# Turning the local pairs' attention probabilities with VectorE blocks and DMA instead of TensorE transposes, in a two-layer hybrid encoder kernel

## The reference

```python
s = einsum('bhcd,ibhcjd->bhcij', q_row, k_win) * scale + bias   # local attention, per grid row
p = softmax(s over the window)
ya = einsum('bhcij,ibhcjd->bhcd', p, v_win) * silu(ag)
x = x + concatenate([ya, yb, yc]) @ w_out
```

## Time and profile before

| | us |
|---|---|
| median of 3 runs | 532.09 (531.93 to 534.18) |
| the profiled execution | 532.22 |
| its span | 530.2 |
| TensorE busy in it | 519.1 (98%) |
| VectorE, ScalarE, POOL busy | 369.8, 279.3, 135.5 |
| SP's queue, POOL's queue: share of the 16 DMA engines | 17.8%, 51.6% |

### The profile page before, as it was taken

One profiled execution on the slowest core, in us unless ns is written; L12 is line 12 of the kernel. 1 busy time (PEld: TensorE's weight loads), 2 busy tenths in 40 slices (PEclk: granted clock), 3 DMA queues, 4 the chain that ended last, 5 costly groups with the idle time before them and its releaser, 6 DMA issues.

```text
span 530.2 us, 7797 instructions
## 1 busy us (share of the span) xinstructions
PE 519.1 (98%) x2846; PEld 406.2 (77%) x2846; DVE 369.8 (70%) x721; ACT 279.3 (53%) x535; POOL 135.5 (26%) x168
## 2 busy tenths in 40 slices
PE   8999999999999999999999999999999999999995
PEld 6888777587786887888888877877768678777884
DVE  6979697989984627611539969979999646546134
ACT  6713376565765558623423315756657656654314
POOL 0114232122133312324411233122122352123201
PEclk9999999999999999999999999999999999999999
DMA  8625688766675875799502479975785969669963
GB/s 285 270 79 138 158 196 203 164 168 160 151 194 137 216 176 117 182 279 269 155 6 99 108 168 217 205 174 133 169 185 137 229 163 253 133 133 231 229 139 159
DMA packets 39014, 92.32 MB, mean 174 GB/s; under 512 B 5440, under 2 KB 16960, under 8 KB 38976
## 3 DMA queue, kind: packets, MB, share of 16 engines
q0 software_dynamic: 17856, 61.09, 51.6%
q1 hardware_dynamic: 20832, 30.54, 17.8%
q10 hardware_dynamic: 288, 0.19, 0.1%
HBM read 81.84 MB, written 4.72 MB: 163 GB/s over the span
## 4 chain that ended last, share of the span: by engine, by line
PE 79%; DMA 9%; DVE 6%; issue 2%; SPq 1%; ACT 1%; POOL 1%; POOLq 0%; DVEq 0%; ACTq 0%
PE acc L560 17%; PE acc L562 17%; PE acc L561 17%; PE tp L684 5%; PE misc L703 4%; PE sc L670 4%; DMA sq<-sq 3%; DMA w_hi<-w_in 2%; DMA bias<-nabias 1%; PE sc L622 1%; PE sc L623 1%; PE sc L624 1%; DMA v_way<-vB 1%; PE sc L560 1%; PE sc L562 1%
## 5 line engine op out<-in xcount | busy, mean ns | idle before, releaser
L560 PE MATMUL acc<-act_hi,w_hi 128*128 128x512 f32 x480 | 195.2, 407 | 0.0
L562 PE MATMUL acc<-act_lo,w_hi 128*128 128x512 f32 x480 | 187.7, 391 | 0.0
L561 PE MATMUL acc<-act_hi,w_lo 128*128 128x512 f32 x480 | 187.3, 390 | 0.0
L562 PEld LDWEIGHTS acc<-act_lo,w_hi 128*128 128x128 f32 x480 | 90.1, 188 | 20.0
L560 PEld LDWEIGHTS acc<-act_hi,w_hi 128*128 128x128 f32 x480 | 90.2, 188 | 17.8 <-issue 1.4
L561 PEld LDWEIGHTS acc<-act_hi,w_lo 128*128 128x128 f32 x480 | 90.5, 188 | 17.0 <-issue 0.5
L783 ACT ACTIVATE w_lo<-w_hi 128x1024 fp32r<-128x1024 f32 (+1 forms) x62 | 61.9, 999 | 42.1 <-DMA w_hi<-w_out 37.3
L846 ACT ACTIVATE prob<-prob,nmx 128x512 f32<-128x512 f32 (+1 forms) x80 | 50.5, 631 | 38.6 <-DVE nmx L1226 38.6
L1206 DVE SCALAR_TENSOR_TENSOR y<-ub,par,y 128x512 f32<-128x512 f32 x90 | 67.3, 748 | 0.0
L1206 DVE SCALAR_TENSOR_TENSOR ub<-ub,par 128x512 f32<-128x512 f32 x84 | 65.8, 783 | 0.0
L1002 POOL DMA_DIRECT2D w_lo<-w_in x40 | 35.8, 895 | 113.1 <-ACT w_lo L783 112.4
(11 more groups left out here) (143 smaller groups left out, 726.1 us busy)
## 6 DMA issues: line engine op xcount, KB each, us to landing
w_hi<-w_in POOLq DMA_DIRECT2D x40, 512.0 KB, 5.1
w_lo<-w_in POOLq DMA_DIRECT2D x40, 512.0 KB, 6.3
w_hi<-w_out POOLq DMA_DIRECT2D x16, 512.0 KB, 6.5
w_lo<-w_out POOLq DMA_DIRECT2D x16, 512.0 KB, 6.6
pT<-w_in SPq DMA_DIRECT2D x15, 512.0 KB, 5.3
bias<-nabias SPq DMA_DIRECT2D x32, 128.0 KB, 4.2
sq<-sq SPq DMA_DIRECT2D x48, 64.0 KB, 2.8
v_way<-vB SPq DMA_DIRECT2D x8, 256.0 KB, 3.1
```

What stands on the lines that cost most here:

```text
L560: nc.tensor.matmul(to[:, :], w_hi[:, slot, k, :], a_hi[:, k, :], start=i == 0, stop=False)
L561: nc.tensor.matmul(to[:, :], w_lo[:, slot, k, :], a_hi[:, k, :], start=False, stop=False)
L562: last = nc.tensor.matmul(to[:, :], w_hi[:, slot, k, :], a_lo[:, k, :], start=False, stop=i == K - 1)
```

## The change

The transposes of the 16 local units leave TensorE. VectorE transposes each unit's 128 x 256 probabilities in blocks of 32 x 32 (`turn_p`, one instruction per unit, in the slot in which TensorE turned it), into `prob[:, 2:4]` or `sq`. For each batch of four units 16 DMAs (32 partitions x 1 KB each) put the blocks on the partitions where they belong, in `pT`: 8 from SP's queue and 8 from POOL's, in slots 30 to 45, two each per slot; those of slots 41 on stand after the loops, on POOL among the weight loads (those of the last batch behind the load_lo that follows tile N_IN+1). `empty_turn` falls away for the local units. values of pair 3 moves from slot 34 to slot 39. values of pair 4 moves into the output projection: in layer 0 after 7 k-blocks of output tile 0 and 4 of output tile 1 (then 3 more of tile 1, then the last k-block of both), in layer 1 between the second and third part of the rows. y's block 1 is now last in K_ORDER. move_x(0) goes behind all this on SP's queue. On ScalarE the negated copies of output tiles 2 and 3 (chunks 34, 35; in layer 1 also 36) stand ahead of the last y_hi.

```diff
-K_ORDER = [2, 3, 4, 0, 5, 6, 1, 7]
+K_ORDER = [2, 3, 4, 0, 5, 6, 7, 1]
...
-Y_BEFORE_W = 6
+W_BEFORE_Y = [1, 2]
...
+        LAST_PAIR = ROW_PARTS[2]
...
+        P_MOVES = {30 + 4 * q + i: (q, i) for q in range(LOCAL // BATCH) for i in range(QUADS)}
+        P_MOVED = 16 * QUADS * QUADS // 2
+        PV_LOCAL = 39
         X_BLOCKS = {26: 0}
-        X_MOVES = {27 + i: (0, i) for i in range(QUADS)}
...
+        def p_turned(q):
+            return (sq if q % 2 else prob[:, 2:4, :])[:, :, :].rearrange("p r t -> p (r t)")
+        def p_there(q):
+            return pT[:, :, :, :].rearrange("p r a t -> p (r a t)")[:, BATCH * NKEY * q:BATCH * NKEY * (q + 1)]
... SP
+            def move_p(l, q, i):
+                sp.wait_ge(p_blocks, LOCAL * l + BATCH * (q + 1))
+                sp.wait_ge(pv_done, PAIRS * l + DPAIRS)
+                for j in range(QUADS // 2):
+                    sp.dma_start(p_there(q)[BLK * j:BLK * (j + 1), NKEY * i:NKEY * (i + 1)],
+                                 p_turned(q)[BLK * i:BLK * (i + 1), NKEY * j:NKEY * (j + 1)]).then_inc(p_moved[q], 16)
...
-                    if l == LAST and n in X_MOVES:
-                        move_x(*X_MOVES[n])
+                    if n in P_MOVES:
+                        move_p(l, *P_MOVES[n])
+                for n in range(UNITS, max(P_MOVES) + 1):
+                    move_p(l, *P_MOVES[n])
                 if l == LAST:
+                    for i in range(QUADS):
+                        move_x(0, i)
... TensorE
-                pe.wait_ge(pt_ready, UNITS * l + UPP * (g + 1))
+                if g < DPAIRS:
+                    pe.wait_ge(pt_ready, DUNITS * l + UPP * (g + 1))
+                else:
+                    for q in range(UPP // BATCH * (g - DPAIRS), UPP // BATCH * (g - DPAIRS + 1)):
+                        pe.wait_ge(p_moved[q], P_MOVED * (l + 1))
+                        pe.wait_ge(p_moved_too[q], P_MOVED * (l + 1))
...
-                                                        pT[:, BLK * i // HD, half, b * P:(b + 1) * P],
+                                                        there[:, 2 * (b % 2) + BLK * i // HD, half],
...
+                    if n == PV_LOCAL:
+                        values(l, DPAIRS)
-                    if LAG <= n < UNITS + LAG:
+                    if LAG <= n < DUNITS + LAG:
                         turn(l, n - LAG)
...
                     for half, kps in ROW_PARTS:
+                        if (half, kps) == LAST_PAIR:
+                            values(l, PAIRS - 1)
                         row_products(half, kps)
...
+                for c, first, end in ((N_IN + CT, 0, KD - 1), (N_IN + CT + 1, 0, KD // 2), (N_IN + CT + 1, KD // 2, KD - 1)):
+                    if first:
+                        values(l, PAIRS - 1)
+                    else:
+                        open_tile(l, c)
+                    products(c, act_hi, act_lo, first, end, order=K_ORDER, ready=(ylo_ready, KD * l))
+                for c in range(N_IN + CT, N_IN + CT + 2):
+                    products(c, act_hi, act_lo, KD - 1, KD, order=K_ORDER, ready=(ylo_ready, KD * l))
... ScalarE
-                    if n > LAG:
+                    if LAG < n <= DUNITS + LAG:
                         empty_turn(l, n - LAG - 1)
...
-                    if i == Y_BEFORE_W - 1:
-                        split_next(l, N_IN + CT - 1)
+                    if i == KD - 2:
+                        for c in range(N_IN + CT - 1, N_IN + CT + W_BEFORE_Y[l]):
+                            split_next(l, c)
... POOL (its move_p: the same with j in 2, 3 and p_moved_too)
+                    if n in P_MOVES:
+                        move_p(l, *P_MOVES[n])
                 for c in range(N_IN, N_CH):
                     hi_next(l, c)
                     lo_next(l, c)
+                    if c == N_IN:
+                        move_p(l, *P_MOVES[UNITS + 1])
+                    if c == N_IN + 1:
+                        for n in range(UNITS + 2, max(P_MOVES) + 1):
+                            move_p(l, *P_MOVES[n])
... VectorE
+            def turn_p(l, n):
+                dve.wait_ge(p_ready, UNITS * l + n + 1)
+                q, u = divmod(n - DUNITS, BATCH)
+                if n == DUNITS:
+                    dve.wait_ge(t_ready, DUNITS * (l + 1))
+                if u == 0 and q >= 2:
+                    dve.wait_ge(p_moved[q - 2], P_MOVED * (l + 1))
+                    dve.wait_ge(p_moved_too[q - 2], P_MOVED * (l + 1))
+                to = p_turned(q).rearrange("p (j u h t) -> p u h j t", j=QUADS, u=BATCH, t=BLK)[:, u]
+                nc.vector.transpose(to, p_of(n).rearrange("p (h j t) -> p h j t", j=QUADS, t=BLK)).then_inc(p_blocks, 1)
...
-                    if n > UPP + LAG and n % UPP == LAG + 1 and n < SLOTS - 1:
+                    if DUNITS + LAG <= n <= UNITS:
+                        turn_p(l, n - LAG)
+                    if n > UPP + LAG and n % UPP == LAG + 1 and n <= DUNITS + LAG + 1:
                         gated(l, n // UPP - 1)
+                    if n == PV_LOCAL + 1:
+                        gated(l, DPAIRS)
+                        turn_p(l, UNITS - 1)
```

More of the change, by code:

```diff
@@ L103 @@
 X_GROUPS = [(0, 1), (1, 2), (2, 3), (3, 5), (5, 6), (6, 8)]
-X_ORDER = [list(range(KD))] + [K_ORDER] * (DEPTH - 1)
+X_ORDER = [list(range(KD))] + [[2, 3, 4, 0, 5, 6, 1, 7]] * (DEPTH - 1)
 WARM = 10
@@ L248, in build @@
         p_ready = sem("p_ready")
+        p_blocks = sem("p_blocks")
+        p_moved = [sem(f"p_moved{q}") for q in range(LOCAL // BATCH)]
+        p_moved_too = [sem(f"p_moved_too{q}") for q in range(LOCAL // BATCH)]
         t_ready = sem("t_ready")
@@ L678, in turn @@
                 pe.wait_ge(p_ready, UNITS * l + n + 1)
-                if UNITS * l + n:
-                    pe.wait_ge(pt_ready, UNITS * l + n)
-                blocks = QT if g < DPAIRS else NKEY // P
-                for k in range(blocks):
+                if DUNITS * l + n:
+                    pe.wait_ge(pt_ready, DUNITS * l + n)
+                for k in range(QT):
                     last = nc.tensor.transpose(tp[:, k * P:(k + 1) * P],
@@ L706, in values @@
                     for b in range(QT):
+                        there = p_there(UPP // BATCH * (g - DPAIRS) + b // 2).rearrange("p (i u h t) -> p u h i t", i=QUADS,
+                                                                                    u=BATCH, t=BLK)
                         for half in range(2):
@@ L762, in _ @@
                         norm_bc(l, MISC_LBC, 2 * l + 2)
-                values(l, PAIRS - 1)
                 if l == LAST:
                     for half, kps in ROW_PARTS:
+                        if (half, kps) == LAST_PAIR:
+                            values(l, PAIRS - 1)
                         row_products(half, kps)
                     break
-                c = N_IN + CT
-                open_tile(l, c)
-                products(c, act_hi, act_lo, order=K_ORDER, ready=(ylo_ready, KD * l))
-                for c in range(N_IN + CT + 1, N_CH):
+                for c, first, end in ((N_IN + CT, 0, KD - 1), (N_IN + CT + 1, 0, KD // 2), (N_IN + CT + 1, KD // 2, KD - 1)):
[6 more added lines that the diff above has]
+                    products(c, act_hi, act_lo, KD - 1, KD, order=K_ORDER, ready=(ylo_ready, KD * l))
+                for c in range(N_IN + CT + 2, N_CH):
                     open_tile(l, c)
-                    products(c, act_hi, act_lo, order=K_ORDER, used=act_used if c == N_CH - 1 else None)
+                    products(c, act_hi, act_lo, order=X_ORDER[l + 1], used=act_used if c == N_CH - 1 else None)
         @block.scalar
@@ L1030, in rotate, with move_p @@
                 nc.gpsimd.tensor_tensor(zsw, zsw, cs[:, 1, :], ALU.mult).then_inc(t2_ready, 1)
+            def move_p(l, q, i):
+                pool.wait_ge(p_blocks, LOCAL * l + BATCH * (q + 1))
+                pool.wait_ge(pv_done, PAIRS * l + DPAIRS)
+                for j in range(QUADS // 2, QUADS):
+                    pool.dma_start(p_there(q)[BLK * j:BLK * (j + 1), NKEY * i:NKEY * (i + 1)],
+                                   p_turned(q)[BLK * i:BLK * (i + 1), NKEY * j:NKEY * (j + 1)]).then_inc(p_moved_too[q], 16)
             nc.gpsimd.memset(ident[:, :], 0.0).then_inc(consts, 1)
```

34 lines of the change are left out of this document (18 added, 16 removed).

## The result

The changed kernel takes 537.55 us (median of 6 runs, 535.68 to 541.71), the kernel before beside it 531.63: a ratio of 1.0111 with an interval of 1.0066 to 1.0156. The forecast was 529.0 and the range ended at 533.6, so the prediction failed in its sign too. Six runs differ by 6 us. The slowest had a mean granted clock of 0.987, the fastest (535.68) one of 0.999, the kernel before 0.998: even a run with almost no lowered clock was 4 us slower than the kernel before. The profiled execution is the one of 541.71 (span 539.8).

The account below looks back on a forecast made before the run. TensorE, busy 519.1 of 530.2 us, was taken as the bound. From 532.2, layer 1's gain of 3.6 and layer 0's loss of 0.4 gave 529.0 us; own range 527.0 to 531.0, 8-in-10 range 525.0 to 533.6.

Parts of the forecast that it names:

- Layer 0, slots 34 to 36: Bias table issued 191.0, landing in 6.8 us, puts maxima(35) at 197.8, slot 36 at 200.65; 1.05 us gained of 5.2.
- A turn at 0.245 us: Each local turn leaving TensorE saves 0.245 us; 16 per layer give 3.9 us.
- I take 0.3: Layer 1, slot 36: loss of 0.3 us, with maxima(35) at 450.91 and its bank freed at 453.8.
- Rival 2: Bias chain binds in both layers, a table 4 us later in layer 1: 532.6 to 533.6, no change; chance 0.17.
- What a wait costs: Layer 0: TensorE waits 2 to 4 us ahead of scores(36) or slot 36; in layer 1 almost none.
- The output phase at 0.9 and 0.8: Losses: 0.9 us in layer 0 for (a), (b), (c); 0.8 in layer 1 for load_lo of output tile 3.
- (a): Layer 0, output tile 0: third k-block's y_lo ends 1.5 us after slot 42, wanted after 1.36; 0.2 to 0.3 us.
- (b): Layer 0, after pair 4's values: three k-blocks (2.05 us) cover its gated, y_hi, y_lo; 0.2 us if nothing is queued ahead.
- (c): Layer 0: tile 28's emptying in slot 40 leaves its bank some 0.2 us of slack; output tile 1's load_lo about as tight.
- POOL's issues: 32 move issues per layer on POOL at 0.6 us each; two per slot fit in slots 30 to 41.
- c: Time of one move's issue on POOL, taken as 0.6 us; past the bound for slower from 1.0 on.
- rival 3: Slower: POOL's move issues hold up the output phase's weights, 532.5 to 538.5 us; chance 0.15.

Follow-up runs that it names:

- e1: Changed kernel with pair 4's value loads on SP's queue at slot 34 instead of 32; 530.04 us, ratio 0.9975.
- e13: Changed kernel with four bias buffers instead of two and idle buffers for batches 2 and 3; 527.78 us, ratio 0.9931.
- e12: Kernel before with four bias buffers and nothing else; 530.42 us, ratio 0.9978.
- e7: e2 with only the change's new order of the output phase, no moves, all turns on TensorE; 533.94 us, ratio 1.0051.
- e2: Kernel before with pair 4's value loads at slot 34 instead of 32; 530.61 us, ratio 0.9977.
- e3: e1 with all 16 moves of each layer's last batch on SP's queue, none on POOL's; 536.56 us, ratio 1.0101.
- e4: e1 with x's first 16 DMAs of layer 1 back in slots 27 to 30 of SP's queue; 534.01 us, ratio 1.0043.
- e8: e2 with pair 3 alone turned by VectorE's blocks and moves, pair 4 by TensorE; 530.88 us, ratio 0.9995.
- e15: Changed kernel with idle buffers for batches 2 and 3, two bias buffers kept; 537.60 us, ratio 1.0103.
- e6: e2 with TensorE waiting in layer 0 ahead of scores(36) for two small DMAs in a row; 537.72 us, ratio 1.0120.
- e9: Changed kernel with four bias buffers instead of two; 537.44 us, ratio 1.0110.
- e10: e8 with four bias buffers; 528.75 us, ratio 0.9949.

## Why the prediction was wrong, step by step

- *Layer 0, slots 34 to 36*: the wait and its place were right, the closeness of the times (maxima(35) at 197.78 for 197.8, slot 36 at 200.55 for 200.65) was luck: the table was issued at 192.26 and not at 191.0, as the V loads went out later and took longer, and landed in 5.4 us and not in 6.8. The transposes took 0.426 us for 0.40, and values was not slowed by its pieces (273 ns a matmul, 1.95 us in all, as in the earlier trace rows).
- *A turn at 0.245 us*: mis-sized. Two slots without turns take 203.50 - 197.98 = 5.52 us in e1, 2.76 each, against 2.97 with one. e13 waits for nothing in layer 1's slots, and from layer 1's norm to the end of slot 42 it is 3.4 us shorter than e12 (199.56 for 202.94). So a turn is worth 0.21, sixteen 3.4 and not 3.9. Why it is less than two turns in a row gave isn't shown.

```profile
197.98 0.47 PE L597 MATMUL acc<-act_hi,w_hi 128*128 128x512 f32 x1 [1.41 <-DVE y L1165]
```
```profile
203.50 0.45 PE L597 MATMUL acc<-act_hi,w_hi 128*128 128x512 f32 x1
```

- *"I take 0.3"* for slot 36 in layer 1, from 6.5 us of slack: the step that failed. I kept maxima(35) at its old place ("450.91 + 2.85 = 453.8") with TensorE 4.2 us earlier, and had nothing in the sum for the two moves ahead of its table (1.6 us) or for a longer landing (2.4 us). maxima(35) came 4.0 us later, and TensorE waited 1.9 + 1.5 us. Rival 2 named this mechanism ("a table 4 us later") and priced it at the lost gain alone.
- *What a wait costs*: a missing term. I forecast some 2.7 us of waiting ahead of scores(36) of layer 0 and over 1 ahead of slot 36 and counted them at their length. Half clock behind them took 1.7 us there and 2.9 in layer 1, where no sum had a wait of that size. It goes only in part with what sets one run of the changed kernel apart from another: the three runs of 538.6 to 541.7 had clocks of 0.987 and 0.988, but 535.68 had 0.999 and 535.74 had 0.992. The run at 0.999 was still 6.7 us over the forecast, so the forecast's sign would have failed without the clock.
- *The output phase at 0.9 and 0.8*: too low. In layer 0 it was 2.9 us longer than before (e7's is 1.8 us longer than e2's without a move). In layer 1 it waited 2.8 us for w_lo. I had looked at y's chain, (a) and (b), and not at the landing of the first output tile's w_lo, which values had covered; (c) names output tile 1's load as "about as tight" and gives it no term of its own. In layer 1 the 0.8 stood for output tile 3's w_lo; the wait of 2.4 us came at the last part, whose w_lo is the last of the queue. Output tile 3's load_hi, which I let land in 6.6 us, did so in 6.2; output tile 4's, issued 1.1 us later, took 11.4. Why the last one was late isn't shown.
- *POOL's issues*: 496 to 909 ns by the row below, but they overlap (8 in 4.3 us, 0.53 each), so c was near the forecast's 0.6 and rival 3 didn't come about; e3 doesn't speak for it either. That its 532.5 to 538.5 takes in the median is luck.

```profile
L1084 POOL DMA_DIRECT2D pT<-prob x32: 496/850/909, 179.1 to 478.1; - x32
```

The sum, against the profiled execution (us longer than in the kernel before; a stage ends where slot 42 does, by the starts of the matmuls):

| | forecast | measured | missed by |
|---|---|---|---|
| layer 0 to the end of slot 42 | -0.5 | 1.1 | 1.6 |
| layer 0's output phase | 0.9 | 2.9 | 2.0 |
| layer 1 to the end of slot 42 | -3.6 | 2.8 | 6.4 |
| layer 1's output phase and the end | 0.0 | 2.9 | 2.9 |

That is 12.9 for the 12.7 between 529.0 and 541.7. The first row is the half clock (1.7), the third the half clock (2.9), slot 36 (1.9 + 1.5 - 0.3 = 3.1) and the turns' price (16 x 0.035 = 0.6). The second and fourth are the output phases; of what fills them, e7 shows 1.8 us of layer 0's as the order's own, and the rest isn't taken apart by a run.

## What to carry to other kernels

When work leaves the bound engine, what it runs into is what was queued late on other engines: before pricing a gain, list everything behind the same blocked queue entry. Two waits that end together hide each other, and here only removing both showed the gain. An event's old time isn't a safe estimate when work is queued ahead of what it waits for, even if its slack is large. Price an idle stretch of TensorE like those here (1.9 us and more in one, or two of over 1 us close together) at its length and a possible half-clock stretch behind it. A piece of work moved away from the front of a stage may have been the cover of a transfer; read what it covered before moving it.

## What the runs showed of the hardware

Ahead of the program's end the traces have six stretches at half clock of 3.4 us (layer 0 of the changed kernel, e1, e3, e4, e8, e15) and three of 6.8 (its layer 1, e6, e9), each with an idle stretch of TensorE just ahead of it or around its start; this time is counted as busy. The landing of a DMA in the same place of the program isn't steady: a store of 256 KB over SP's queue landed in 4.4 us in layer 1 of the kernel before and in 7.1 in the changed one, but in layer 0 it took 7.1 in the kernel before too, and the medians of eight are 3.1 and 3.2. So that the moves beside it lengthened it isn't shown. Small DMAs of 32 KB took 0.59 us to issue on SP and 0.53 on POOL back to back. POOL's closing instruction took 3.7 to 7.0 us, and in e3, e8 and e10 it ended the run after the last output had landed.
